# One transpose of x for all, and a first quarter of q, k, v and gate together

## The reference, cut to what matters

```
mod = silu(c) @ ada_w + ada_b                 # 2048 x 12288: shift, scale, gate of mixer and FFN
h = rmsnorm(x, norm_mix_g) * (1 + scale_m) + shift_m
q, k, v, g, gk, cq, ckv, kr, ga, gb = split(h @ w_in)      # widths 1024 1024 2048 2048 16 512 512 64 2048 2048
log_a = log_sigmoid(gk @ gla_gk_w + gla_gk_b) / 16
o = gated_linear_attention(q, k, v, log_a)
y_gla = (rmsnorm(o) * silu(g)) @ gla_wo
... latent attention from cq, ckv, kr; merge with sigmoid(ga), sigmoid(gb); w_out; SwiGLU FFN; two layers of the second block
```

## Time and profile before

| what | value |
|---|---|
| median of 3 runs | 2657.13 us (2656.78 to 2657.72) |
| profiled execution: its own time, first to last instruction | 2656.8 us |
| PE busy | 2569.4 us, 97% |
| DVE, ACT, POOL busy | 1718.7, 1303.5, 76.9 us |
| mean granted clock of PE | 0.996 |
| DMA | 554.27 MB, mean 209 GB/s |

### The profile page before, as it was taken

The page is one execution under the profiler, slowest core; times in us unless marked ns, Lnnn a source line. Parts: engine busy times, 40 slices in busy tenths (PEclk is TensorE's granted clock), DMA queues, the critical chain, the costliest instruction groups (busy, mean ns, idle before and its releaser), DMA issues.

```text
span 2656.8 us, 35508 instructions
## 1 busy us (share of the span) xinstructions
PE 2569.4 (97%) x12983; PEld 2181.5 (82%) x12983; DVE 1718.7 (65%) x2262; ACT 1303.5 (49%) x1900; POOL 76.9 (3%) x116
## 2 busy tenths in 40 slices
PE   3989999999999999999999999999999999999999
PEld 3888887888887887888888888889888888888887
DVE  6877776776766756677655555566656655566664
ACT  3345455434555445444443444455654545565553
POOL 0000000000000000000000000002000101100000
PEclk9999999999999999999999999999999999999999
DMA  9975665887676765787666666566465465555564
GB/s 365 348 247 159 187 202 175 303 298 265 210 246 198 234 211 169 248 264 259 223 198 192 186 186 183 188 191 190 146 190 173 136 215 149 174 177 175 148 201 134
DMA packets 325063, 554.27 MB, mean 209 GB/s; under 512 B 24462, under 2 KB 135804, under 8 KB 324252
## 3 DMA queue, kind: packets, MB, share of 16 engines
q1 hardware_dynamic: 319104, 541.79, 64.1%
q0 software_dynamic: 3168, 7.12, 0.8%
q10 hardware_dynamic: 2620, 3.09, 0.3%
HBM read 549.83 MB, written 2.10 MB: 208 GB/s over the span
## 4 chain that ended last, share of the span: by engine, by line
PE 90%; DVE 4%; ACT 3%; issue 2%; DMA 1%; SPq 0%; POOL 0%; DVEq 0%; ACTq 0%
PE gp L825 82%; PE tp L825 5%; PE tp L828 2%; DMA raw_first<-in_ada_w_dram 1%; ACT whi L1260 1%; DVE wlo L1883 1%; DVE acc L1889 0%; ACT L1260 0%; DVE xs L1883 0%; ACT hraw L1260 0%; SPq L808 0%; DVE stat L2207 0%; ACT sx L1260 0%; DVE sx L1883 0%; DVE yd L1883 0%
## 5 line engine op out<-in xcount | busy, mean ns | idle before, releaser
L1883 DVE TENSOR_TENSOR wlo<-raw,whi 128x1024 fp32r<-128x1024 f32 (+1 forms) x830 | 983.2, 1197 | 641.0 <-ACT whi L1260 637.4
L1260 ACT ACTIVATE whi<-raw 128x1024 fp32r<-128x1024 f32 (+1 forms) x830 | 848.2, 1036 | 607.3 <-PE gp L825 483.6
L825 PE MATMUL gp<-whi,h 128*128 128x512 f32 (+1 forms) x2944 | 928.8, 387 | 6.1 <-DVE wlo L1883 4.6
L825 PEld LDWEIGHTS gp<-whi,h 128*128 128x128 f32 x2944 | 550.8, 188 | 107.6 <-issue 10.4
L825 PE MATMUL gp<-h,whi 128*128 128x512 f32 (+1 forms) x1936 | 605.5, 372 | 24.7 <-DVE wlo L1883 10.9
L825 PE MATMUL gp<-wlo,h 128*128 128x512 f32 (+1 forms) x1472 | 560.4, 381 | 0.0
L825 PE MATMUL gp<-h,wlo 128*128 128x256 f32 x1680 | 474.8, 283 | 0.0
L825 PEld LDWEIGHTS gp<-h,whi 128*128 128x128 f32 x1936 | 352.7, 192 | 96.4 <-issue 20.4
L825 PEld LDWEIGHTS gp<-h,wlo 128*128 128x128 f32 x1680 | 320.5, 191 | 0.8 <-issue 0.7
L825 PEld LDWEIGHTS gp<-wlo,h 128*128 128x128 f32 x1472 | 277.6, 189 | 45.2 <-issue 1.0
L1889 DVE SCALAR_TENSOR_TENSOR acc<-raw,cact,acc 128x1024 f32<-128x1024 f32 x149 | 190.5, 1278 | 7.4 <-DMA raw<-in_ada_w_dram 6.6
(11 more groups left out here) (333 smaller groups left out, 2640.0 us busy)
## 6 DMA issues: line engine op xcount, KB each, us to landing
raw<-in_w_in_dram SPq DMA_DIRECT2D x310, 512.0 KB, 4.3
raw<-in_ffn_w_in_dram SPq DMA_DIRECT2D x176, 512.0 KB, 4.7
raw<-in_ada_w_dram SPq DMA_DIRECT2D x158, 512.0 KB, 5.0
raw<-in_w_out_dram SPq DMA_DIRECT2D x96, 512.0 KB, 4.3
raw<-in_ffn_w_down_dram SPq DMA_DIRECT2D x88, 512.0 KB, 4.3
raw<-in_w_in_dram SPq DMA_DIRECT2D x64, 384.0 KB, 3.5
raw_first<-in_ada_w_dram SPq DMA_DIRECT2D x34, 512.0 KB, 8.9
raw<-in_gla_wo_dram SPq DMA_DIRECT2D x32, 512.0 KB, 5.7
```

Source lines behind the costliest of these rows:

```text
L825: return e.matmul(o, l, r, start=start, stop=stop)
L1260: return e.activation(o, i, f, **kw)
L1883: return e.tensor_tensor(o, a, b, op)
```

## The change

x is normalised earlier in the list, and all its 16 tiles are transposed at once before the first `ada_mod` (`x_T`, eight groups of four in four steps) into `XT`, which lies in the place of h. `fnorm` has no PE part any more: ACT scales `XT` into `hraw` (`fn_h`).

The first stage of the list now has the first four contraction tiles of all q, k, v and gate blocks: 24 GEMM units, with 24 ada units (pair 1 and half of pair 2) among them. The second has q and k over tiles 4 to 7 (8 GEMM units) and 8 ada units; the third has q and k over tiles 8 to 11 and v blocks 0 and 1 over tiles 4 to 11 (16 GEMM units) and 16 ada units. The fourth has `gk` and the last quarter of q and k (9 GEMM units) and no ada unit. v and gate are finished after it. While a unit of these four stages runs, the preparation goes up to five units ahead in place of three.

Gate blocks are now stored, added to by DVE and then passed through SiLU by ACT from SBUF; the minimum and the subtraction of log_a are one DVE instruction from PSUM, so those four small banks are free only after `gk_sub`. Buffers move to make room.

```diff
-BORDERS = [("fg", 0), ("rvg", 1, 0), ("q", 0, 0), ("q", 0, 1), ("q", 0, 2), ("gk",)]
+BORDERS = [("fg", 0), ("rvg", 1, 0), ("q", 0, 0), ("q", 0, 4), ("q", 0, 8), ("gk",)]
+GLA_FROM = ("v", 0)
...
+    part_of = {}
+    def piece(kind, j, k0, K):
+        o = {"q": o_q, "k": o_k, "v": o_v, "g": o_g}[kind]
+        args = (j,) if k0 + K == KD else (j, k0)
+        job = gemm(kind, args, wcols(w_in, o + 512 * j, 512), K, 512, "h", turned=kind in ("q", "k"), k0=k0, adds=part_of.get((kind, j)))
+        part_of[kind, j] = job["name"]
+        return job
+    qk = [(kind, j) for kind in ("q", "k") for j in range(2)]
+    vg = [(kind, j) for kind in ("v", "g") for j in range(4)]
+    early = [[piece(*x, 0, 4) for x in qk + vg], [piece(*x, 4, 4) for x in qk], [piece(*x, 8, 4) for x in qk] + [piece(*x, 4, 8) for x in vg[:2]]]
...
+    early.append([gk_job] + [piece(*x, 12, 4) for x in qk])
+    for x in vg[:2]:
+        piece(*x, 12, 4)
+    for x in vg[2:]:
+        piece(*x, 4, 12)
...
-    for qd in range(3):
-        mine = [(job, ci) for job in quarters[qd] for ci in range(len(job["chunks"]))]
-        spots = [((i + 0.5) / 16, 0, u) for i, u in enumerate((adas[qd + 1], ci) for ci in range(KD))]
-        spots += [(0.2 + 0.8 * (i + 0.5) / len(mine), 1, u) for i, u in enumerate(mine)]
+    mods = [(adas[seq], ci) for seq in range(1, 4) for ci in range(KD)]
+    for n, (lead, to, ahead) in enumerate(((0.1, 24, 1.0), (0.0, 32, 0.8), (0.0, 48, 0.85), (0.0, 48, 1.0))):
+        mine = [(job, ci) for job in early[n] for ci in range(len(job["chunks"]))]
+        now = mods[(0, 24, 32, 48)[n]:to]
+        spots = [(ahead * (i + 0.5) / len(now), 0, u) for i, u in enumerate(now)]
+        spots += [(lead + (1.0 - lead) * (i + 0.5) / len(mine), 1, u) for i, u in enumerate(mine)]
...
-        while prep < min(n + LOOK + 1, len(chunks)):
+        while prep < min(n + (5 if chunks[n]["first"] and n >= KD else LOOK) + 1, len(chunks)):
...
-        return [idle] * 2 + [step(("x_sq", (), 0)), step(("rows", (), 1))] + [idle] * 4 + [step(("x_ss", (), 0)), idle] + \
-            [step(("x_norm", (t,), 0)) for t in range(2)]
+        return [idle] * 2 + [step(("x_sq", (), 0)), step(("rows", (), 1))] + [idle] * 2 + [step(("x_ss", (), 0)), idle] + \
+            [step(("x_norm", (0,), 0), ("x_norm", (1,), 0))] + [step(("x_T", (2 * n,), 1), ("x_T", (2 * n + 1,), 1)) for n in range(4)]
...
-        return [step(("fn_T", (2 * j,), 1), ("fn_T", (2 * j + 1,), 1), need=[("start",)]),
-                step(("fn_hi", (2 * j,), 0), ("fn_hi", (2 * j + 1,), 0), *([("gla_loads", (), 0)] if j == 3 else no))]
+        return [step(("fn_h", (2 * j,), 0), ("fn_hi", (2 * j,), 0), need=[("start",)]),
+                step(("fn_h", (2 * j + 1,), 0), ("fn_hi", (2 * j + 1,), 0), *([("gla_loads", (), 0)] if j == 3 else no))]
...
         def gk_sub(us, t):
             w.wait_ge(gk_ln_done, t + 1)
-            for u in uses["gk_la", t]:
-                w.wait_ge(tp_dve[u.b], at("tpd", *u))
-            tt(LOGA[:, t, :], LMIN[:, t, :], LOGA[:, t, :], ALU.subtract).then_inc(loga_done, 1)
+            for n, u in enumerate(uses["gk_la", t]):
+                la = LOGA[:, t, n * 512:(n + 1) * 512]
+                stt(la, full(u)[:, :], 0.0, la, ALU.min, ALU.subtract).then_inc(tp_dve[u.b], 1)
+                note(tp_dve[u.b], "tpd", *u)
```

More of the change, by code:

```diff
@@ L261, in make_jobs @@
     n = 64
-    rest = [(job, ci) for job in jobs if job in quarters[3] or not job["chunks"][0]["first"] for ci in range(len(job["chunks"]))]
+    rest = [(job, ci) for job in jobs if not job["chunks"][0]["first"] for ci in range(len(job["chunks"]))]
     late = [u for u in rest if u[0]["name"] == ("ymla", 0) and u[1] == 7]
@@ L702, in program @@
     RAW_FIRST = [w1("raw_first0", 24, [3, 2, 512]), w1("raw_first1", 69, [3, 2, 512])]
[L703 to L706, removed]
+    XT = place("xt", h_off, [KD, 2, S])
+    hraw = w1("hraw", 36, [2, 2, S])
+    posi, posf = w1("posi", 85.5, [4], I32), w1("posf", 85.625, [4])
+    lamv, ang, nrnd = w1("lamv", 40, [2, 4, 64]), w1("ang", 1, [2, 128]), w1("nrnd", 2, [2, 128])
+    junk = [w1(f"junk{l}", 3 + 0.5 * l, [2, 64]) for l in range(2)]
     LOGA = w1("loga", 0, [2, 1024])
@@ L925, in gla_sum @@
             (u,) = us
-            w.wait_ge(loga_done, 2)
+            for t in range(2):
+                for v in uses["gk_la", t]:
+                    taken_dve(v)
             w.wait_ge(d_lvl, 32)
@@ L1240, in unit @@
             last.then_inc(mm_done, 1)
-        parts = dict(rows=rows, warm=warm, ada_mod=ada_mod, ada_out=ada_out, fn_T=fn_T, gk_la=gk_la, gk_kr=gk_kr, gk_krt=gk_krt,
+        parts = dict(rows=rows, warm=warm, ada_mod=ada_mod, ada_out=ada_out, x_T=first_T, gk_la=gk_la, gk_kr=gk_kr, gk_krt=gk_krt,
                      gla_sum=gla_sum, gla_sc=gla_sc, gla_av=gla_av, gla_og=gla_og, lat_T=lat_T, pr_qn=pr_qn, pr_kn=pr_kn, pr_rr=pr_rr, pr_sc=pr_sc,
@@ L1364, in ada_out, with x_T, fn_h @@
             note(tp_act[u.b], "tpa", *u)
+        def x_T(us, pair):
+            (u,) = us
+            bk = full(u)
+            copy(XT[:, 2 * pair:2 * pair + 2, 1, :], tok_pairs(bk[:, :])).then_inc(tp_act[u.b], 1)
+            note(tp_act[u.b], "tpa", *u)
+        def fn_h(us, pair):
+            m = first_use("ada_mod", pair // 2)
+            w.wait_ge(tp_dve[m.b], at("tpd", *m))
+            u = first_use("x_T", pair)
+            w.wait_ge(tp_act[u.b], at("tpa", *u))
+            if pair >= 2:
+                w.wait_ge(h_hi, at("h", "h", pair - 2))
+                w.wait_ge(h_lo, at("h", "h", pair - 2))
+            for n in range(2):
+                k = 2 * pair + n
+                fn(hraw[:, pair % 2, n, :], XT[:, k, 1, :], ACT.Identity, scale=modc[:, 1, k:k + 1], bias=modc[:, 0, k:k + 1]).then_inc(h_raw, 1)
         def norm_T(u, pair, hr, scale, shift, was):
@@ L1375, in norm_T, with norm_hi @@
             note(tp_act[u.b], "tpa", *u)
-        def norm_hi(u, pair, hr, was):
-            w.wait_ge(tp_act[u.b], at("tpa", *u))
+        def norm_hi(pair, hr, was):
             copy(HH[:, 2 * pair:2 * pair + 2, :], hr[:, pair % 2, :, :]).then_inc(h_hi, 1)
             note(h_hi, "h", was, pair)
[L1382 to L1385, removed]
         def fn_hi(us, pair):
-            norm_hi(first_use("fn_T", pair), pair, hraw, "h")
+            w.wait_ge(h_raw, 2 * pair + 2)
+            norm_hi(pair, hraw, "h")
         def t_sin(us):
@@ L1712, in evac @@
             kind, args, g, N = job["kind"], job["args"], no % 2, job["N"]
+            if kind in ("ygla", "ymla", "dn", "xo") or kind == "g" and len(args) == 1:
+                after_dve(job)
+                return
             if job["adds"]:
-                return
-            if kind in ("ygla", "ymla", "dn", "xo"):
-                after_dve(job)
                 return
@@ L1749, in evac @@
                 return
-            elif kind == "v":
-                read(first_use("fn_T", 2 * args[0]))
-                read(first_use("fn_T", 2 * args[0] + 1))
+            elif kind in ("v", "g"):
+                if kind == "v":
+                    read(first_use("x_T", 2 * args[0]))
+                    read(first_use("x_T", 2 * args[0] + 1))
                 for n in range(2):
[L1754 to L1759, removed]
+                    copy((V if kind == "v" else SG)[:, n, args[0] * 512:(args[0] + 1) * 512], ps[n][:, :]).then_inc(gp_act[g], 1)
             elif kind in ("cq", "ckv"):
                 st, ss, rs = STG[0 if kind == "cq" else 1], scol(2, "lat_ss", kind), scol(2, "lat_rs", kind)
-                w.wait_ge(loga_done, 2)
+                first_read()
                 for n in range(2):
@@ L1838, in after_dve @@
             kind, args = job["kind"], job["args"]
+            if kind == "g":
+                sg = SG[:, :, args[0] * 512:(args[0] + 1) * 512]
+                w.wait_ge(gp_dve[job["no"] % 2], at("gpd", "g", args[0]))
+                fn(sg, sg, ACT.Silu).then_inc(sg_done, 1)
             if kind == "fg":
```

63 lines of the change are left out of this document (22 added, 41 removed).

## The result

| | median, us | lowest to highest | ratio to before, 95% interval |
|---|---|---|---|
| before | 2657.43 | 2656.78 to 2658.32 (4 runs) | |
| after | 2667.22 | 2665.77 to 2668.68 (4 runs) | 1.0036 [1.0024, 1.0049] |

The changed kernel is slower by 9.8 us; 2656.0 was predicted, with 2638 to 2667. Its profiled execution spans 2666.7 us against 2656.8 us. The first line is part one of the page after, as the earlier trace rows: PE's busy time, instructions and share hardly moved, so the page alone doesn't say where 10 us went.

The account below looks back on a forecast made before the run. PE, busy 97%, was taken as the bound. Losses of 28.4 us before against 1.5 + 2.4 + 3.4 + 20.0 = 27.3 us after gave 1.1 us less: 2656.0 us, range 2638 to 2667.

Parts of the forecast that it names:

- Transposes: 24 of the 32 transposes leave the GEMM stretch: 3.0 us less on PE.
- The waits at the borders before: Kernel before, first GEMM to end of quarter 2: 14.5 us of PE waits, mostly at the borders of the quarters.
- Start: Before the first GEMM: it starts at 49.0, not 47.54, so 1.5 us lost, with bounds 0 to 3 us.
- The slow start: First 48 matmuls, which took 8.28 us where two units need 5.76: a loss of 2.4 us that stays.
- Third stage: First half: DVE has 31 us against PE's 23.0; PE waits six times under 1 us, 3.4 us; bounds 0 and 8.
- the rival that I gave 0.15: Third stage: DVE's excess is not covered, the lead being under about 1 us; 2665 us, slower; chance 0.15.
- Fourth stage: Preparation five units ahead with four `whi` slots: 13.3 us of waits plus 6.7 us at lower clock, 20.0 us.
- q's first wait: Fourth stage: q's first unit needs v block 1's banks, its addition standing behind a preparation; PE idle 3.6 us.
- The slow stretches: Fourth stage: each of the three long waits is followed by a lower clock, about 2.2 us each, 6.7 us.
- Later: After the fourth stage: additions, stored pieces, later SiLU and moved ada units lie beside PE's work and cost nothing.
- Transfers: Rival: transfers set the pace; at 320 GB/s the last unit comes 12 us late, 2668 us; chance 0.08.
- The signs: No PE gap over 1 us from 50 to 190 us, third `ada_mod` about 190, then gaps about 3.6, 3.5, 4.5.

Follow-up runs that it names:

- e4_xT_only: The kernel before with only the transposes made once and early, and `fn_h` scaling from `XT`: 2655.57 us, ratio 0.9992.
- e8_start: e2_cap with the lead of three units kept up to unit 19 and five from unit 20 on: 2645.40 us, ratio 0.9952.
- e2_cap: The kernel after, preparing up to five units ahead, but a GEMM unit never more than three GEMM units ahead: 2647.62 us, ratio 0.9963.
- e13_all: e2_cap with e5_silu, e6_swap and e8_start, and the rope tables made beside `gk` instead of in the third stage: 2631.16 us, ratio 0.9898.
- e5_silu: e2_cap with the gate's SiLU taken out of the evacuation and made an ACT step of its own: 2645.44 us, ratio 0.9951.
- e6_swap: e2_cap with two neighbours in the unit list, ada unit 186 and ckv unit 187, exchanged: 2644.17 us, ratio 0.9950.

## Why the prediction was wrong, point by point

- **Transposes, 3.0 us: fits, not shown alone.** They have left PE's part of the list; in e4_xT_only longer border waits take back half, in after there are no such waits.
- **The waits at the borders before: right.** After has 0.4 us idle in the first two stages.
- **Start, 1.5 us: 2.2 us**, inside the bounds of 0 to 3 us, by another way than I wrote. PE did reach full speed (`ada_mod` 1.84 us and not 3.4), which should have made it nearly nothing; the copy for unit 21 took it back, and e8_start shows that it would have been a gain. I had not listed the copies that the longer lead puts ahead of `fn_h`. The slow start cost 1.6 us in place of 2.4.
- **Third stage, 3.4 us: it lost 8.7 us. This step failed.** The count of DVE's work, 51 us against 45 of PE, was right to 3 us (48.15 busy). The step's mistake was to cover 3.4 of 8 us of excess by the lead and to spread the rest over six waits under 1 us: they were 3.05, 0.42, 0.19 and 2.22, and a stretch at the lower clock followed, so that the stage lost even more than my upper bound of 8. The lead was there, some 5 us at the stage's start (the `wlo` that begins at 138.58 ends at 139.8, and PE starts that unit at 145.1). It was eaten in one place, by 4.7 us of tables and `acc` between two `wlo` and by 1.80 us of DVE's waiting for ACT, which I had put at nothing. So it isn't the rival that I gave 0.15 either, whose condition was a lead under 1 us; that its 2665 us lies near the measured 2667 is luck, since it has nothing for the loss further on and 12.6 us for this stage.
- **Fourth stage, 20.0 us: 18.7 us, and right in mechanism**: the rows of ACT and DVE show the copy in front of the `evac`, and e2_cap, with fewer GEMM units ahead, removes it; that the number of slots sets the step stays argued. The waits came to 11.1 us for 13.3: `gk_la` 3.87 for 3.5, k 0.86 for 0.7, `gk_kr` 4.42 for 4.5, `gla_sc` 0.99 for 1.0. q's first wait was 0.95 for 3.6, because I took `gk` for one unit, in the prediction and in the description of the kernel; it is two (so the stage has ten GEMM units, not nine), and the second one covers v's addition. The slow stretches cost 7.6 us for 6.7, which made up for part of it: that the total is so near is in part luck.
- **Later, nothing: it lost 5.7 us. This step failed, and is the largest miss.** I had counted DVE's and ACT's busy time beside PE's and found room. The room was there, 179.38 of 245.00 us busy on DVE. What I had not done is what I did for the fourth stage: go through the list. Two places make most of it: SiLU behind DVE's addition, with the exponent of level 7 behind it (2.19 us and a slow unit), and an ada unit that now falls between `gla_av(3, 1)` and `gla_og(0)`, so that PE has no GEMM unit to run while DVE gates (2.53 us and a slow unit). With both mended, in e13_all, the stretch from `gla_sc` to `ygla` takes 225.1 us and not 234.8; before, less the six units that have moved, it was 229.0.
- **Transfers: no sign.** No wait of PE between 50 and 640 us is ended by a DMA; that rival's 2668 us is near the measured time by chance.
- **The signs.** "No PE gap over 1 us between 50 and 190 us" failed, by 3.05 and 2.22 us. "The third `ada_mod` about 190" came true, 190.56, and proves nothing: from a first GEMM at 49.0 my own terms give 184.8 for it, so the stage's extra loss is what brought it to 190.

Together: third stage 5.3, later 5.7, start 0.7, a short wait in the first two stages 0.4, slow start -0.8, fourth stage -1.3: 10.0 us over the forecast of -1.1 us makes +8.9; the spans differ by 9.9. Of the 1.0 us left, 0.8 lie behind 480 us, in no single place that I found.

## What to carry to other kernels

Count a prefetch lead in what it takes up, not in list positions: preparations for more units than there are slots wait for the consumer, and all that stands behind them in the same engine's list waits too. Where an engine's work in a stage exceeds PE's, move a piece out of the stage, not about in it: here the one gave 6 us and the other nothing. And look for two engines waiting for each other, which idles the busy one. Spare busy time on an engine doesn't cover an operation that now waits for another engine; go through the order on each queue at every place where a wait is added or a cover is taken out.

## What the runs showed of the hardware

The wait of 3.87 us was followed by this window of the kernel after, at a granted clock of 0.50 (1.2 of 2.4 GHz) though PE was busy all through:

```profile
214.30:222.00 7.70, 7.70 (x23) 5.15 (x24) 0.00 (x0) 0.00 (x0) 0.00 (x0) 0.50 0.00 0
```

Behind the waits of 2.22, 4.42, 2.19 and 2.53 us the clock was low too; behind the three under 1 us of the fourth stage it was at 1.00. What a low clock cost behind the waits of 2.2 and 2.5 us is the 1.5 to 1.7 us by which the stretches of after, e2_cap and e8_start differ. But a long wait doesn't always bring it. The same wait at the same place of the list, in after (first) and in e2_cap:

```profile
157.20:160.40 3.20, 3.06 (x24) 2.85 (x24) 3.20 (x4) 1.65 (x2) 0.00 (x0) 1.00 0.69 191
```

```profile
157.80:161.00 3.20, 3.20 (x15) 3.20 (x16) 3.20 (x4) 1.70 (x2) 0.00 (x0) 0.50 0.63 190
```

After 3.05 us of waiting PE went on at full clock, caught up with DVE and waited 2.22 us more at 169.28; after 3.06 us it went on at half, and the wait at that place was 0.56 us. From one `ada_mod` to the next the stage took 52.9 us both ways, with DVE as its bound: here the slow stretch cost nothing. e5_silu and e6_swap have e2_cap's lists up to there, and behind the same 3.06 us one went on at 0.50, the other at 1.00. This fits what the Trainium skill says (TensorE: Matmul & The Clock Gate, Part 1: the monitor runs freely, so the place of a change varies from run to run), though the traces are of different kernels and none shows the monitor itself. I had weighed that page against the long waits of the fourth stage, and there the low clock did come.
